# A two-layer diffusion block on one core: order of the out-projection chunks, the context's modulation, and how the probabilities are turned

## The reference, cut to what matters

```python
attend:     s = q_nope.k_nope + q_rope.k_rope          # per head
            p = softmax(s * SM_SCALE);  out = p @ v
mixer_out:  merged = g_a * (attn @ w_ao) + g_f * (four @ w_fo)
            return merged @ w_out                      # the out projection
layer:      x   = ln_affine(ALPHA * x + gate1 * mixer_out(...), ln1_g, ln1_b)
            ctx = the same with its own gate           # first layer only
            f   = swiglu(layer_norm(x) * (1 + scale2) + shift2)   # layer 0; ctx too
            x   = ln_affine(ALPHA * x + gate2 * f, ln2_g, ln2_b)
```

## Time and profile before

| | us |
|---|---|
| median of three executions | 2315.37 |
| the three | 2315.37, 2316.22, 2303.54 |
| the profiled execution | 2310.37 |
| its span, first to last instruction | 2308.2 |
| outside the span | 2.2 |

### The profile page before, as it was taken

The page is one execution under the profiler, slowest core; times in us unless marked ns, Lnnn a source line. Parts: engine busy times, 40 slices in busy tenths (PEclk is TensorE's granted clock), DMA queues, the critical chain, the costliest instruction groups (busy, mean ns, idle before and its releaser), DMA issues.

```text
span 2308.2 us, 33336 instructions
## 1 busy us (share of the span) xinstructions
PE 2090.3 (91%) x13189; PEld 1440.2 (62%) x13189; DVE 970.8 (42%) x1450; ACT 751.1 (33%) x1007; POOL 603.1 (26%) x346
## 2 busy tenths in 40 slices
PE   6988889997999999988888589999999999998886
PEld 3454457776877778854576456666565666666654
DVE  2234432267222346744324644333443333445545
ACT  2034542234222234234433232223332223334442
POOL 0012222251112224112224013333222333233441
PEclk8999999999999999999899689999999999999997
DMA  7210115452254445411166068999978999989993
GB/s 273 96 42 19 37 37 166 171 173 92 92 181 167 144 139 190 144 41 37 54 220 237 24 266 340 401 400 417 387 274 338 395 402 421 385 323 410 419 421 148
DMA packets 158815, 514.85 MB, mean 223 GB/s; under 512 B 8492, under 2 KB 72108, under 8 KB 115524
## 3 DMA queue, kind: packets, MB, share of 16 engines
q1 hardware_dynamic: 158660, 512.69, 58.5%
HBM read 511.61 MB, written 1.05 MB: 222 GB/s over the span
## 4 chain that ended last, share of the span: by engine, by line
PE 71%; issue 9%; DVE 8%; POOL 5%; DMA 3%; ACT 3%; SPq 0%; DVEq 0%; POOLq 0%; ACTq 0%
PE psum L842 68%; POOL w_lo L2764 3%; POOL reg_p L2741 1%; DVE w_lo L2075 1%; PE psum L1126 1%; DMA ring<-in_w_mod 1%; DVE stat L2284 1%; ACT w_hi L1640 1%; DMA ring<-in_w_out 1%; DVE reg_q L2277 1%; DMA ring<-in_w_in 1%; ACT lat_q L1654 1%; DMA e_ring<-in_experts 0%; POOL w_lo L2718 0%; PE psum L1539 0%
## 5 line engine op out<-in xcount | busy, mean ns | idle before, releaser
L2764 POOL TENSOR_TENSOR w_lo<-e_ring,w_hi 128x512 fp32r<-128x512 f32 x92 | 217.7, 2368 | 530.4 <-PE psum L842 337.8
L2718 POOL TENSOR_TENSOR w_lo<-ring,w_hi 128x512 fp32r<-128x512 f32 (+1 forms) x88 | 202.2, 2299 | 561.9 <-ACT w_hi L1640 561.9
L842 PE MATMUL psum<-e_ring,reg_q 128*32 128x128 f32 (+3 forms) x4272 | 302.5, 332 | 11.6 <-issue 3.4
L2075 DVE TENSOR_TENSOR w_lo<-ring,w_hi 128x1536 fp32r<-128x1536 f32 (+1 forms) x88 | 161.4, 1839 | 338.2 <-ACT w_hi L1640 338.1
L1640 ACT ACTIVATE w_hi<-ring 128x2048 fp32r<-128x2048 f32 (+1 forms) x88 | 161.2, 1834 | 353.7 <-DMA ring<-in_w_in 84.4
L842 PEld LDWEIGHTS psum<-e_ring,reg_q 128*32 128x32 f32 (+1 forms) x4272 | 182.1, 120 | 117.0 <-issue 66.1
L2075 DVE TENSOR_TENSOR w_lo<-e_ring,w_hi 128x1536 fp32r<-128x1536 f32 x92 | 170.7, 1858 | 160.8 <-PE psum L842 135.0
L1979 ACT ACTIVATE w_hi<-e_ring 128x2048 fp32r<-128x2048 f32 x92 | 175.7, 1911 | 176.6 <-DMA e_ring<-in_experts 174.4
L842 PE MATMUL psum<-h_hi,w_hi 128*128 128x512 f32 (+1 forms) x400 | 149.6, 374 | 11.4 <-issue 11.4
L842 PE MATMUL psum<-reg_q 96*128 96x512 f32 (+4 forms) x300 | 130.2, 561 | 19.1 <-ACT reg_v L1805 10.1
L842 PE MATMUL psum<-h_lo,w_hi 128*128 128x512 f32 (+1 forms) x400 | 147.3, 368 | 0.0
(11 more groups left out here) (306 smaller groups left out, 3761.9 us busy)
## 6 DMA issues: line engine op xcount, KB each, us to landing
e_ring<-in_experts SPq DMA_DIRECT2D x240, 1024.0 KB, 9.6
e_more<-in_experts SPq DMA_DIRECT2D x96, 1024.0 KB, 9.7
ring<-in_w_mod SPq DMA_DIRECT2D x48, 1024.0 KB, 7.8
ring<-in_w_in SPq DMA_DIRECT2D x22, 1024.0 KB, 5.3
ring<-in_w_ff_down SPq DMA_DIRECT2D x22, 1024.0 KB, 5.0
ring<-in_w_out SPq DMA_DIRECT2D x12, 1024.0 KB, 5.0
ring<-in_w_ff_gate SPq DMA_DIRECT2D x11, 1024.0 KB, 5.3
ring<-in_w_ff_up SPq DMA_DIRECT2D x11, 1024.0 KB, 5.4
```

What stands on the lines that cost most here:

```text
L842: ins = pe.matmul(o, lhs, rhs, start=start, stop=stop, **kw)
L2075: return dve.tensor_tensor(dst, src, hi.bitcast(F32), ALU.subtract)
L2718: pool.tensor_tensor(w_lo[:, n % SLOTS, a:size], ring[:, n % SLOTS, a:size], w_hi[:, q % HIS, a:size].bitcast(F32), ALU.subtract).then_inc ...
L2764: pool.tensor_tensor(lo_slot[slot][:, LO_DVE:SLOT], e_slot[slot][:, LO_DVE:SLOT], w_hi[:, (n_split + t) % HIS, LO_DVE:SLOT].bitcast(F32), ...
```

## The change

It has three parts.

1. The four out-projection chunks of half 1 come with the channel half outermost: (0,0), (1,0), (0,1), (1,1). Their PSUM banks are 4 to 7 for the latents and 0 to 3 for the context, and the waits for free banks move with them.
2. The context's two tiles are modulated by ACT (four channel blocks, bank 6) and DVE (the other four, bank 7) into `h_ctx`, a buffer of its own for each tile. The first context tile is turned in the middle of the chunk (1,0), the second behind it. DVE's and ACT's lists are written in another order around it: the splits of the gate/up chunks come later, the context's second pair of residuals earlier.
3. POOL no longer multiplies the tile of probabilities. It writes a 128x128 matrix with the inverse sums on its diagonal (`p_inv`, three buffers), and PE multiplies each block of `reg_p`, as the stationary operand, by it in place of the transpose.

```diff
--- before.py
+++ after.py
@@ -268,8 +268,7 @@
                 mod(l, MERGE_MOD[u])
         v = w["w_out"][l].rearrange("(g k p) n -> g p k n", k=4, p=P)
         for half in OUT_HALVES[l]:
-            for dh in range(2):
-                for kk in range(2):
+            for dh, kk in OUT_CHUNKS[half]:
                     chunks.append((("out", l, half, dh, kk), [(0, (4, 512), v[kk, :, :, dh * 512:(dh + 1) * 512])]))
         if l == 0:
             for fp in range(FT // 2):
@@ -298,6 +297,7 @@
 
 
 OUT_HALVES = ((1, 0), (1,))
+OUT_CHUNKS = (((0, 0), (0, 1), (1, 0), (1, 1)), ((0, 0), (1, 0), (0, 1), (1, 1)))
 IN_ORDER = ((0, 1, 2, 3), (0, 2, 3, 1))
 
 MERGE = [(kind, jj) for kind in ("ga", "gf", "ao", "fo") for jj in range(4)]
@@ -384,6 +384,7 @@
         c_act = ctx.enter_context(nc.sbuf_tensor("c_act", [P, KD, 32], F32))
         modcol = ctx.enter_context(nc.sbuf_tensor("modcol", [P, DEPTH, 4, KD, 2], F32))
         stat = ctx.enter_context(nc.sbuf_tensor("stat", [P, 80], F32))
+        p_inv = ctx.enter_context(nc.sbuf_tensor("p_inv", [P, 3, P], F32))
         bn = stat[:, 0:12].rearrange("p (a b) -> p a b", a=2)
         ln_mv = stat[:, 12:20].rearrange("p (n a) -> p n a", a=2)
         ln_std = stat[:, 20:24]
@@ -479,6 +480,7 @@
         lo_slot = [w_lo[:, i, :] for i in range(E_SLOTS)] + [v[:, :] for v in lo_more]
 
         h_mod = lat_q
+        h_ctx = reg_q[:, 8192:10240].rearrange("p (t n) -> p t n", t=2)
         z_of = [None, reg_q[:, 8192:10240].rearrange("p (b n) -> p b n", b=2),
                 reg_f[:, :].rearrange("p (b n) -> p b n", b=2), z_sb, z_sb]
         xn_2 = nc.alloc_sbuf_tensor_at("xn_2", [P, 2, D], F32, offset=at_lat)
@@ -726,9 +728,7 @@
             return (xn if use == 2 and t < 2 else xn_of[use])[:, t % 2, :]
 
         def out_bank(l, t, dh):
-            if l == 0 and t < 2:
-                return 2 + 2 * dh + t
-            return 4 - 4 * dh + t % 2
+            return (4 if t >= 2 else 0) + 2 * dh + t % 2
 
         def ff_bank(t, dh):
             return (4 if t >= 2 else 0) + 2 * (t % 2) + dh
@@ -1123,9 +1123,8 @@
                         pe.wait_ge(t_out, 64 * l + c - 1)
                     nt = 2 if s == 0 else 4
                     for k in range(nt):
-                        ins = pe.transpose(psum[:, 4 + c % 2, k * P:(k + 1) * P], reg_p[:, c % 3, k * P:(k + 1) * P],
-                                           ident)
-                    ins.then_inc(t_mm, 1)
+                        mm(psum[:, 4 + c % 2, k * P:(k + 1) * P], reg_p[:, c % 3, k * P:(k + 1) * P], p_inv[:, c % 3, :],
+                           start=True, stop=True, sig=t_mm if k == nt - 1 else None)
 
                 def pv(u):
                     g, pair, s = units[u]
@@ -1192,29 +1191,28 @@
 
                 pe.wait_ge(mod_done, mod_at[(l, 11)] + 1)
                 for half in OUT_HALVES[l]:
-                    for dh in range(2):
-                        if half == 1 and dh == 1:
-                            pe.wait_ge(g_mul, 16 * l + 16)
-                        if half == 0 and dh == 1:
-                            pe.wait_ge(y_read, 2)
-                        for kk in range(2):
-                            v = split_chunk(("out", l, half, dh, kk), (4, 512))
-                            pe.wait_ge(mlo_ok, 4 * l + 2 * kk + 2)
-                            for t in (2 * half, 2 * half + 1):
-                                cols = slice(t * P, (t + 1) * P)
-                                for k in range(4):
-                                    last = kk == 1 and k == 3
-                                    kc = 4 * kk + k
-                                    mm3(psum[:, out_bank(l, t, dh), :], (m_hi[:, kc, cols], m_lo[:, kc, cols]),
-                                        [x[:, k, :] for x in v], start=(kk == 0 and k == 0), stop=last,
-                                        sig=y_mm if last else None, free=w_used if t % 2 and k == 3 else None)
-                                if half == 0 and dh == 1 and kk == 1:
-                                    turn_tile(1, t, 2 + t)
+                    if half == 0:
+                        pe.wait_ge(g_mul, 16 * l + 16)
+                    for dh, kk in OUT_CHUNKS[half]:
+                        v = split_chunk(("out", l, half, dh, kk), (4, 512))
+                        pe.wait_ge(mlo_ok, 4 * l + 2 * kk + 2)
+                        for t in (2 * half, 2 * half + 1):
+                            cols = slice(t * P, (t + 1) * P)
+                            for k in range(4):
+                                last = kk == 1 and k == 3
+                                kc = 4 * kk + k
+                                mm3(psum[:, out_bank(l, t, dh), :], (m_hi[:, kc, cols], m_lo[:, kc, cols]),
+                                    [x[:, k, :] for x in v], start=(kk == 0 and k == 0), stop=last,
+                                    sig=y_mm if last else None, free=w_used if t % 2 and k == 3 else None)
+                            if half == 0 and dh == 1 and kk == 1:
+                                if t == 0:
+                                    pe.wait_ge(y_read, 4)
+                                turn_tile(1, t, 2 + t)
 
             def dense_mixer():
                 first = [(0, 0), (0, 1), (1, 0)]
 
-                def gate_up(fp, m, cols, end):
+                def gate_up(fp, m, cols, end, between=None):
                     v = split_chunk((("fg", "fu")[m], fp), (KD, 256))
                     for i in range(2):
                         if fp >= 1 and (fp, m) not in first:
@@ -1225,17 +1223,17 @@
                                 [x[:, k, i * P:(i + 1) * P] for x in v], (h_hi[:, k, cols], h_lo[:, k, cols]),
                                 start=(k == 0), stop=last, sig=(fg_mm, fu_mm)[m] if last and end else None,
                                 free=w_used if last and i == 1 and end else None)
+                        if i == 0 and between is not None:
+                            between()
 
                 pe.wait_ge(ht_act, tiles_before[1] + 2)
                 pe.wait_ge(ht_dve, tiles_before[1] + 2)
-                pe.wait_ge(y_read, 4)
+                pe.wait_ge(y_read, 6)
                 gate_up(0, 0, slice(CTX, NTOK), False)
-                pe.wait_ge(y_read, 6)
+                pe.wait_ge(y_read, 8)
                 gate_up(0, 1, slice(CTX, NTOK), False)
-                pe.wait_ge(y_read, 8)
-                gate_up(1, 0, slice(CTX, NTOK), False)
-                for t in range(2):
-                    turn_tile(1, 2 + t, t)
+                gate_up(1, 0, slice(CTX, NTOK), False, lambda: turn_tile(1, 2, 0))
+                turn_tile(1, 3, 1)
                 pe.wait_ge(ht_act, tiles_before[2])
                 pe.wait_ge(ht_dve, tiles_before[2])
                 for fp, m in first:
@@ -1880,13 +1878,22 @@
                     std(n + 2)
                     std(n + 3)
                     modulate(0, 2, 2, at)
+                    modulate(0, 2, 3, at + 1)
                     split_hi(q_ffn + 1)
-                    modulate(0, 2, 3, at + 1)
                     split_hi(q_ffn + 2)
                     for i in range(4):
                         std(n + 4 + i)
-                    modulate(0, 2, 0, at + 2)
-                    modulate(0, 2, 1, at + 3)
+                    for t in range(2):
+
+                        act.wait_ge(xn_turned[0], at + t + 3)
+                        for k in range(4):
+                            ins = act.activation(h_ctx[:, t, k * P:(k + 1) * P], psum[:, 6, k * P:(k + 1) * P],
+                                                 ACT.Identity, bias=modcol[:, 0, 2, k, 0:1],
+                                                 scale=modcol[:, 0, 3, k, 0:1])
+                        link(ins)
+                        act.wait_ge(y_read, 9 + t)
+                        act.activation(h_hi[:, :, t * P:(t + 1) * P],
+                                       h_ctx[:, t, :].rearrange("p (k n) -> p k n", k=KD), ACT.Copy).then_inc(ht_act, 1)
 
                 if l == 0:
                     for fp in range(FT // 2):
@@ -2371,17 +2378,25 @@
                     add_mixer(0, 0)
                     add_mixer(1, 0)
                     modulate(0, 2, 2, at)
-                    split_lo(q_ffn + 1)
-                    modulate(0, 2, 3, at + 1)
                     add_mixer(0, 1)
                     add_mixer(1, 1)
+                    modulate(0, 2, 3, at + 1)
                     norm_a(1, 0, 2, n + 4)
-                    split_lo(q_ffn + 2)
+                    split_lo(q_ffn + 1)
                     norm_a(1, 1, 3, n + 5)
                     norm_b(1, 0, 2, n + 6)
+                    split_lo(q_ffn + 2)
                     norm_b(1, 1, 3, n + 7)
-                    modulate(0, 2, 0, at + 2)
-                    modulate(0, 2, 1, at + 3)
+                    for t in range(2):
+                        dve.wait_ge(xn_turned[1], at + t + 3)
+                        for k in range(4, KD):
```

(13 more changed lines are left out.)

## The result

The changed kernel takes 2294.91 us (median of 8 runs, 2289.95 to 2297.12) against 2309.01 before (8 runs, 2303.54 to 2316.22). The ratio is 0.9938, 95% interval 0.9922 to 0.9954: 14.3 us faster (10.6 to 18.0). The profiled execution took 2293.47 us with a span of 2291.6, which is 16.6 us less than the span before.

A forecast was written before the change was run, and what follows sets the result against it. PE was taken to bound the dense mixer, the chain through DVE, POOL and PE's transposes the attentions. +11.4 - 4.5 - 5 = +1.9 us on 2310.37 gave 2312; the forecast was 2313 us, range 2296 to 2330.

The forecast's parts named there:

- On the path: Both attentions: passes added on the chain, +20.2 us, less POOL's shorter multiplications, -8.8 us, make +11.4 us.
- 174 x 0.116: Both attentions: 174 of 320 blocks lie on the chain, each costing one more PE pass of 0.116 us: +20.2 us.
- the low clock goes: Rival, both attentions: products and shorter waits keep the clock up, about 16 us come back, 2297 us; chance 0.18.
- The 21 us lost to the clock: Both attentions: PE's loss while working at the lower clock level, 14 us in layer 0 and 7 in layer 1.
- -8.8 forecast: Both attentions: POOL writes 128 columns, saving 0.10 us on 10 small and 0.31 on 25 large chain operations.
- four passes: Rival, both attentions: a block's product takes four records of 0.116 us, +42 us in all, 2354 us; chance 0.03.
- -4.5 forecast: Layer 0 out projection: the 4.0 us wait goes, one of 2.0 us comes; between -5.1 and -2.1 us.
- if it drops again: Layer 0 out projection: third chunk ends at about 511.3 if the clock drops, 508.3 if it stays; before 513.4.
- -5 forecast: Layer 0 seam: from the latents' to the context's gate/up pairs 26.4 us in place of 31.3.
- every pass counts: Rival, both attentions: all 320 passes land on the path with nothing back, +27.5 us, 2339 us; chance 0.10.
- the seam gives nothing: Rival, layer 0 seam: third chunk's weights and DVE's two splits replace the removed waits, 2321 us; chance 0.09.
- +11.4 and -9.5: Attention term of part 3, +11.4 us; out-projection order and seam terms of parts 1 and 2, -4.5 and -5 us.

The follow-up runs named there:

- filler in the waits: Kernel before, with PE transposing the identity once per block (320 overwritten passes) ahead of its wait for POOL's result: 2302.38 us.
- transposed twice: Kernel before, with each block of probabilities transposed twice into the same place, POOL as before: 2308.03 us.
- transposed three times: Kernel before, with each block of probabilities transposed three times, POOL as before: 2329.66 us.
- product with the identity: Kernel before, with each block turned by a product with the plain identity in place of the transpose, POOL as before: 2312.1 us.
- short POOL, transposes: Kernel before, transposes kept, POOL writing only the 128 columns of p_inv, which nobody reads, so probabilities stay unscaled: 2292.14 us.
- part 3 alone: Kernel before with only the diagonal product on PE and POOL writing the 128 columns of p_inv: 2301.07 us.
- `p_inv` on DVE, without / with the split moved: Changed kernel with DVE writing p_inv behind its reciprocal: 2283.57 us; also with DVE's split of (1,0) ahead of the context's first norm_b: 2282.33 us.
- the two kernels with products: Kernel before with blocks multiplied by the plain identity, POOL as before, 2312.1 us; and with the diagonal product and short POOL operation, 2301.07 us.
- the last run above: Changed kernel with p_inv written by DVE and DVE's split of (1,0) moved ahead of the context's first norm_b: 2282.33 us.
- the run before it: Changed kernel with p_inv written by DVE right behind its reciprocal, the split of (1,0) not moved: 2283.57 us.
- the two kernels without part 3: Kernel before with part 2 of the change only, 2312.66 us; and the changed kernel with part 3 undone, 2302.62 us.

## Why the prediction was wrong

**The attentions in numbers.** I take each one's length from the starts in the traces: in layer 0 from PE's first work on `reg_p` to its first on `g_hi`, in layer 1 from DVE's first on `stat` to the same. Kernels with an untouched attention are the kernel before, part 1, part 2, and both.

| kernel | layer 0, us | layer 1, us | merge behind layer 1, us |
|---|---|---|---|
| untouched (four profiles) | 160.9, 155.7, 158.3, 157.9 | 108.0, 107.9, 110.8, 110.8 | 124.6, 127.7, 122.9, 120.8 |
| filler in the waits | 157.3 | 107.2 | 122.0 |
| transposed twice | 164.0 | 109.1 | 120.8 |
| transposed three times | 175.3 | 117.4 | 120.3 |
| product with the identity | 164.1 | 112.1 | 122.3 |
| short POOL, transposes | 150.0 | 102.4 | 120.7 |
| part 3 alone / whole change | 159.5 / 161.3 | 105.6 / 105.7 | 119.7 / 120.9 |
| `p_inv` on DVE, without / with the split moved | 156.3 / 156.3 | 101.1 / 101.1 | 119.0 / 119.9 |

**The step that failed** is in part 3, *On the path*: "The old chain stays a path through the new order, so at this clock and these prices less is not to be had." The chain was right and the clock was not given. The third pass costs (175.3 - 164.0) + (117.4 - 109.1) = 19.6 us by the trace, against my 174 x 0.116 = 20.2; the second costs only (164.0 - 158.2) + (109.1 - 109.4) = 5.5 us over the mean of the untouched ones. So about 14 us of the 20 are paid by the clock: with more work between its waits PE has next to no stretches at 1.2 GHz left in the attentions. An estimate from the windows comes out near it. The clock went from 0.925 to 0.98 over 169 us and from 0.91 to 0.99 over 115 us (means of the untouched profiles, then two passes); the differences times the lengths are 18 us, and with PE's busy share there, 0.87, that is 16 us of PE work. I had this as the rival "the low clock goes", worked out at 2297 us, and gave it 0.18. What I held against it, that the waits set by DVE and ACT stay, was true and did not matter. The 21 us lost to the clock should have been weighed against +20 us of PE work in those same stretches. Against the mean of the untouched profiles the whole change made the attention of layer 0 3.1 us longer and that of layer 1 3.7 shorter; I had forecast 8 and 3 longer.

**Its carry.** The merge behind the attention of layer 1 has the same code everywhere, and took 124.0 us on average behind an untouched attention, 120.6 over the eight profiles with more PE passes, filler included. Its clock in the kernel before and the changed one was 0.94 and 0.99:

```profile
1136.00:1260.00 124.00, 108.89 (x812) 95.03 (x812) 38.24 (x45) 38.05 (x44) 37.50 (x18) 0.94 0.65 221
```

```profile
1125.00:1246.00 121.00, 104.23 (x812) 90.47 (x812) 38.95 (x47) 38.04 (x44) 38.07 (x19) 0.99 0.67 226
```

I had no term for it. Part of the gain turns into the longer wait for `m_lo` behind it, 5.41 us where it was 3.65. The stage scatters from 120.8 to 127.7 where nothing was changed, so a mean over four profiles is thin; and the short operation on POOL, without any pass more, has 120.7 too. That the attention's clock causes it was not tested.

**POOL's shorter operation.** The price was right: a median of 0.374 us where I had estimated 0.38, and 0.463 on average with the operations that took up to 1.8 us. Its worth came out higher: -8.8 forecast, 11 us between the two kernels with products by the times (4.6 + 6.5 by the table), which the intervals can't tell from 8.8, and 17 [12, 22] beside transposes, which they can. In layer 0 4.6 us are what I had (4.4); in layer 1 6.5 against 4.3, where all tiles have 512 columns. I had counted 14 of layer 1's 32 operations, those on the old chain; 6.5 us are 19 of them at 0.34 us (0.803 - 0.463). Either others waited too, or the clock, 1.00 there against 0.97, did the rest.

**The kind of instruction.** The runs with two transposes and with a product of two passes have the same clock, 0.98 in layer 0 and 0.99 and 0.97 in layer 1. The Trainium skill, "TensorE: Matmul & The Clock Gate", Part 4, says that the fast clock does not engage for transpose mode, since it does not count as PE being busy in the same way; the durations beside this are for bf16. Here 320 FP32 transposes more lifted the clock as much as products did, so the runs disagree with it. The rival "four passes", by the Trainium skill, "TensorE: Matmul & The Clock Gate", Terms, fell too: 640 records for 320 blocks, at 0.111 us.

**Part 1**, -4.5 forecast: -4.2 timed alone, and 55.4 us in place of 60.2 from the first matmul on `m_hi` to the first on `h_hi`, -4.8. The next wait was forecast at 2.0 us until 502.9; it is 1.79 us until 503.01. The rest hangs on the clock behind that wait. In four of the five profiles with the new order it stays up; in the last run above it fell behind a wait of 3.00 us, 25 matmuls took 8.73 us where the run before it has 5.96, and the stretch took 59.3 us in place of 55.4. That is the case that I had as "if it drops again".

**Part 2**, -5 forecast: 27.06 us in the trace against a working of 26.4, so -4.2 in its place. The new wait for the split of (1,0) is 1.85 us, forecast as 2. In the time of the two kernels without part 3 less arrives: parts 1 and 2 together give -6.0, part 1 -4.2, and 1.8 is left, within intervals of about 4 us. I had let nothing behind the seam take any of it back, and in these two kernels the one longer wait in the experts, by some 5 us, does. The changed kernel doesn't have it.

**The rival "every pass counts"** turned on PE's idle time ahead of the blocks. It did not stay as it was; it fell from 34.9 to 17.2 us.

The rival "the seam gives nothing" named the two new waits rightly, and neither took the place of the whole gain.

**In sum:** -8.8 for part 3 and -6.0 for the others make -14.8, and the whole was -14.3. That the sum comes out so well is in part luck, since the -6.0 were timed with the longer wait in the experts, which the changed kernel doesn't have. The forecast was +11.4 and -9.5. The 20 us of error in part 3 are 14 of clock in the attentions, 2 of POOL (11 against 8.8), and some 3 in the merge behind, within what single profiles can tell.

## What to carry to other kernels

Where PE waits often and the granted clock of a stretch is below 1.00, work added on PE may cost less than its own duration: price it once at constant clock, and once with the low stretches gone, and give both a real chance. A run with useless passes placed ahead of the waits shows cheaply how much there is to win, and a further copy of the added pass shows what it costs once that is spent. A single profile of an untouched stage scattered by 5 us here, so a term of that size needs several profiles or a timed run of its own.

## What was not expected of the hardware

Useless PE work made the kernel faster by 8.5 us [5.8 to 11.3], by what it does to the clock. The low clock may also outlast its stage: the merge behind the second attention was 3.4 us shorter on average where the attention had more passes, though this isn't shown to be the cause. And moving a 128-column operation from POOL (0.463 us on average, up to 1.8) to DVE (0.316 us), behind DVE's own reciprocal, took 8 to 11 us off the changed kernel; by the table the attentions are 9.6 us shorter. On the 35 operations of the chain I had counted, the difference in duration is 35 x 0.147 = 5.1 us; the rest went with the handover between the engines, or with operations off that chain, which no run separates. And one wait of PE in the experts, 3.4 us before, was 8.4 and 8.8 us in two kernels whose edits lie far ahead of it.
